# A hybrid attention block on Trainium2: in the dilated stage, TensorE's transposes move ahead of its score products

## Chip, cores, metric

The kernel runs on one core of one Trainium2 chip. The metric is the device time of one execution in microseconds, as the median of several runs; lower is better.

## What is computed

One layer over 2048 positions of width 1024. A combined input projection feeds two mixers of eight heads each (head size 64) and a gate; their outputs are gated, projected and normalised. The change is in mixer A, the dilated attention. It runs three configurations on each head, (window, dilation) = (128, 1), (512, 4), (2048, 16):

```python
def fold(a):                       # position t = m*dil + r
    a = a.reshape(b, tc, dil, h, dh).transpose(0, 2, 1, 3, 4)
    ...
    return a.reshape(b, dil, nb, BLK, h, dh)
...
s = jnp.einsum('brnqhd,brnkhd->brnhqk', qf, kf) / math.sqrt(dh) + bias
s = jnp.where(valid[:, None], s, -jnp.inf)     # band of 128 keys, causal
m = jnp.max(s, axis=-1, keepdims=True)
p = jnp.exp(s - m)
den = jnp.sum(p, axis=-1)
o = jnp.einsum('brnhqk,brnkhd->brnqhd', p, vf) / den
...
w = softmax over the three configurations of (m + log den)
y = sum of w * o
```

Each tile of 128 queries sees its own block of 128 keys and, unless it is the first of its residue, the block before it.

## The kernel before

The program is four phases one after the other, with a barrier between them: `front_phase` (first norm and most of the input projection), `stick_phase` (mixer B and the rest of the projection), `dilated_phase` (mixer A) and `output_phase`. Each engine has its own instruction list in a phase, written out by hand, and the lists meet only through semaphores.

In `dilated_phase` a head has 48 tiles, 16 for each configuration. `make_bunches` puts them into 20 bunches: the 4 bunches of dilation 16 (four tiles of one key block each), then 8 of dilation 4, then 8 of dilation 1 (two tiles each, with one or two key blocks). A bunch is at most 512 columns of scores. Two heads make a turn of 40 steps (`STEPS`); there are four turns (`PAIRS`), so 160 steps. The first turn is written out, the others are a loop on the engines, and `run_turns` goes through the steps for TensorE, ScalarE and VectorE alike. Below, S(b), T(b), V(b) and so on mean the work for bunch b.

At step s each engine works on several bunches at once (`behind` gives the bunch that lies a lag behind, across turns too):

- **TensorE** (`one_step`, lines 1335 to 1343): the scores S(s) (`scores`, lines 1294 and 1295; two products for each tile, with the queries as weights, read with the dilation as stride), the transposes T(s-2) (`transpose_weights`, line 1303; three or four), the value products V(s-4) (`values`, lines 1320 and 1321; two for each key block). At step 13 of each turn but the first, `transpose_pair` (line 1331) turns the merged output of the turn before.
- **VectorE**: `minima` (line 1418) reads the scores, adds the bias and takes the row minimum of the negated scores; `add_halves` (line 1436) for bunch s-5; `low_part` (line 1428) makes PT_lo(s-2); at step 13 four times `apply_gate` (line 1475), which waits for an earlier store of y.
- **ScalarE**: `copy_low` (line 1375) for bunch s-5; `high_part` (line 1367) makes PT_hi(s-2) from the transposes; `weights` (line 1358) makes the exponentials of bunch s, each followed by a read of its row sum.
- **SyncE** stores and reloads the rows of the dilated configurations, loads the next head and stores y; **GpSimd** merges the three configurations.

The waits that matter here: S(s) waits until `minima` has read bunch s-2 (`min_done`; the scores have two PSUM banks). T(b) waits for the exponentials of bunch b (`exp_done`) and for `low_part` of bunch b-2 (`lo_done`; two banks again). V(b) waits for `low_part` of b. The exponentials of b wait for `minima` of b.

Of the kernel before, what the change touches and what calls it, by code (L numbers as in the profile page):

```python
# [37 lines left out]
def at(it, per_turn, n):  # L38

    return it * per_turn + n  # L40


def behind(it, before, s, steps, lag):


    if s >= lag:
        return (it, s - lag) if s - lag < steps else None
    return None if before is None else (before, s - lag + steps)
# [1044 lines left out]
def dilated_phase(nc, qk_hi_d, qk_lo_d, gate_d, va_d, toe_d, ident, y_d):  # L1093
# [42 lines left out]
    STEPS = TURN_HEADS * NB  # L1136
    OBANKS = 3 * NTILE // 4

    def bank_of(c, idx):

        return ORDER.index(c) * (NTILE // 4) + idx // 4


    LAG_T, LAG_H, LAG_L, LAG_V, LAG_O = 2, 2, 2, 4, 5
# [8 lines left out]
    with ExitStack() as stack:  # L1153
# [43 lines left out]
        def run_turns(eng, one_step):  # L1197

            for s in range(STEPS):
                one_step(0, None, s)  # L1200
            with eng.Fori(1, PAIRS) as it:
                for s in range(STEPS):
                    one_step(it, it - 1, s)
            for s in range(STEPS, STEPS + max(LAG_O, LAST_WEIGH + 2)):
                one_step(PAIRS - 1, None, s)
# [69 lines left out]
        @block.tensor  # L1275
        def _(pe):
            pe.sem_inc(pt_done, SCORE_SLOTS)
            pe.sem_inc(pv_done, PART_SLOTS)
            pe.sem_inc(y_done, NCH)
            pe.wait_ge(q_zeros_set, 2)  # L1280

            def scores(it, b):
                par, bunch = b // NB, BUNCHES[b % NB][0]
                if b % NB == 0:
                    pe.wait_ge(qk_loaded[par], at(it, 16 * HeadTiles.QK_LOADS, 16 * HeadTiles.QK_LOADS))
                pe.wait_ge(min_done, at(it, STEPS, b + 1))
                for c, idx, r, n, nk, col in bunch:
                    d = DILATIONS[c]
                    q0 = r + d * P * n
                    k0 = r + d * P * (n - nk + 1)  # L1290
                    q = slice(q0, q0 + d * (P - 1) + 1, d)
                    k = slice(k0, k0 + d * (nk * P - 1) + 1, d)
                    out = s_ps[b % 2][:, col:col + nk * P]
                    pe.matmul(out, q_hi2[par][:, q], k_both[par][:, k], start=True, stop=False)  # L1294
                    last = pe.matmul(out, q_lo0[par][:, q], k_both[par][:, k], start=False, stop=True)  # L1295
                last.then_inc(s_done, 1)

            def transpose_weights(it, b):
                width = BUNCHES[b % NB][1]
                pe.wait_ge(exp_done, SCORE_SLOTS + at(it, STEPS, b + 1))  # L1300
                pe.wait_ge(lo_done, at(it, STEPS, b + 1))
                for col in range(0, width, P):
                    last = pe.transpose(t_ps[b % 2][:, col:col + P], prob[b % SCORE_SLOTS][:, col:col + P], ident[:])
                last.then_inc(pt_done, 1)

            def values(it, b):
                par, bunch = b // NB, BUNCHES[b % NB][0]
                pe.wait_ge(lo_done, 2 + at(it, STEPS, b + 1))
                for c, idx, r, n, nk, col in bunch:
                    bank = par * OBANKS + bank_of(c, idx)  # L1310
                    if idx == 0:
                        pe.wait_ge(v_loaded[c][par], at(it, 16 * V_LOADS[c], 16 * V_LOADS[c]))
                    if idx % 4 == 0:

                        pe.wait_ge(rows_done, at(it, 2 * OBANKS, bank + 1))
                    out = o_ps[bank % 2][:, (idx % 4) * P:(idx % 4 + 1) * P]
                    for kb in range(nk):
                        w = slice(col + kb * P, col + (kb + 1) * P)
                        vk = v[c][par][:, idx - nk + 1 + kb, :]
                        pe.matmul(out, PT_hi[b % PART_SLOTS][:, w], vk, start=(kb == 0), stop=False)  # L1320
                        last = pe.matmul(out, PT_lo[b % PART_SLOTS][:, w], vk, start=False, stop=(kb == nk - 1))  # L1321
                last.then_inc(pv_done, 1)

            def transpose_pair(pair, last_pair=False):
                pe.wait_ge(merged, 1 + at(pair, 2, 1 if last_pair else 2))
                for ch in range(NCH):
                    if last_pair:
                        pe.wait_ge(last_merged, ch + 1)
                    pe.wait_ge(gated, at(pair, NCH, ch + 1))
                    for j in range(4):  # L1330
                        last = pe.transpose(y_ps[ch % 2][:, j * P:(j + 1) * P],
                                            y_pos[:, ch * 4 + j, :], ident[:])
                    last.then_inc(y_done, 1)

            def one_step(it, before, s):
                if s < STEPS:
                    scores(it, s)
                if then := behind(it, before, s, STEPS, LAG_T):
                    transpose_weights(*then)
                if then := behind(it, before, s, STEPS, LAG_V):  # L1340
                    values(*then)
                if s == PAIR_AT and before is not None:
                    transpose_pair(before)

            run_turns(pe, one_step)
            transpose_pair(PAIRS - 1, last_pair=True)

# [490 lines left out]
```

## Time and profile before

| what | value |
|---|---|
| median of 3 runs | 1833.44 us (1826.37 to 1836.2) |
| the profiled execution, its own time | 1834.93 us |
| its span, first to last instruction | 1833.1 us |
| TensorE busy | 1706.5 us, 93% |
| VectorE busy | 1173.7 us, 64% |
| ScalarE busy | 806.1 us, 44% |
| dilated stage, first to last product of the 160 steps | 1227.34 to some 1619 us of the span |
| mean granted TensorE clock | 0.967 of full |

Times in the trace are microseconds from the start of the span. "Busy" for TensorE is the time in which any matmul is under way; matmuls overlap, so what a matmul costs in a dense stretch is the distance from its start to the next start, and not its duration. PE is TensorE, PEld its weight loads, DVE VectorE, ACT ScalarE, POOL GpSimd, SPq the queue that SyncE issues DMAs on. The span leaves out 1.8 us of the execution's own time.

### The profile page before, as it was taken

What the parts mean: (1) busy time and instruction counts of PE and PEld (TensorE: products, weight loads), DVE (VectorE), ACT (ScalarE), POOL (GpSimd) and SP (SyncE); (2) the same over time, 40 slices, a digit from 0 to 9 for tenths busy, and PEclk for the clock granted to TensorE, in tenths of its full rate; (3) what the DMA queues carried; (4) which work ended last, traced back from release to release, by engine and by line L of the source; (5) the groups of instructions that cost most, each with busy time, mean ns of one, the idle gap of its engine ahead of it and who ended that gap; (6) DMA issues with size and microseconds to landing.
All of it is one profiled execution on the core that took longest, in us unless ns stands there. A gap on an engine that the chain in (4) does not pass through costs nothing. (4 is left out here: it accounts for less than half of the span.)

```text
span 1833.1 us, 27600 instructions
## 1 busy us (share of the span) xinstructions
PE 1706.5 (93%) x9138; PEld 1457.2 (79%) x9138; DVE 1173.7 (64%) x2323; ACT 806.1 (44%) x1993; POOL 194.7 (11%) x172
## 2 busy tenths in 40 slices
PE   5799999999979999999999999959989899959998
PEld 4577888888868888888787888849989899947886
DVE  5531123333238888888888888837667676765996
ACT  3341112222225555555555555538768686742000
POOL 2102100000000000000000000010222222200231
PEclk9899999999989999999999999979989999979999
DMA  4316954666367539465654454259888888446541
GB/s 161 138 66 222 333 193 166 208 200 209 131 188 221 179 124 289 141 179 177 228 178 150 144 157 153 89 140 204 191 213 180 198 183 195 106 135 216 187 151 59
DMA packets 235236, 320.01 MB, mean 175 GB/s; under 512 B 66781, under 2 KB 160408, under 8 KB 231516
## 3 DMA queue, kind: packets, MB, share of 16 engines
q1 hardware_dynamic: 230620, 308.90, 56.5%
q0 software_dynamic: 2400, 9.48, 1.6%
q8 instruction: 63, 1.03, 0.2%
q14 instruction: 73, 0.60, 0.1%
q10 hardware_dynamic: 2080, 0.01, 0.1%
HBM read 208.38 MB, written 109.94 MB: 174 GB/s over the span
## 5 line engine op out<-in xcount | busy, mean ns | idle before, releaser
L1003 ACT ACTIVATE WT_hi<-wt_ps 128x512 fp32r<-128x512 f32 (+1 forms) x320 | 170.9, 534 | 316.3 <-PE wt_ps L935 316.3
L1049 DVE TENSOR_TENSOR_SCAN W<-w,W,zeros 128x512 f32<-128x512 f32 x192 | 248.2, 1293 | 59.3 <-ACT w L995 58.5
L376 PE MATMUL proj<-h_hi,w_hi 128*128 128x512 f32 x640 | 260.2, 407 | 19.2 <-DVE h_lo L552 16.5
L376 PE MATMUL proj<-h_hi,w_lo 128*128 128x512 f32 x640 | 253.2, 396 | 0.0
L376 PE MATMUL proj<-h_lo,w_hi 128*128 128x512 f32 x640 | 252.9, 395 | 0.0
L1358 ACT ACTIVATE prob<-neg_s,rows 128x256 f32<-128x256 f32 (+1 forms) x384 | 173.5, 454 | 51.8 <-DVE rows L1418 47.9
L1057 DVE TENSOR_TENSOR WT_lo<-wt_ps,WT_hi 128x512 fp32r<-128x512 f32 (+1 forms) x320 | 187.4, 586 | 2.2 <-ACT WT_hi L1003 2.2
L1294 PE MATMUL s_ps<-k_both,q_hi 128*128 128x256 f32 (+1 forms) x384 | 151.9, 402 | 38.1 <-DMA q_lo<-qk_lo_d 20.1
L1418 DVE CUSTOM_DVE_ANT_0 neg_s<-s_ps,bias 128x256 f32<-128x256 f32 (+1 forms) x384 | 122.6, 363 | 99.5 <-PE s_ps L1295 89.3
L935 PE MATMUL wt_ps<-ident,W 128*128 128x128 f32 x1088 | 173.5, 275 | 7.0 <-DVE WT_lo L1057 6.2
L995 ACT ACTIVATE w<-z_ps 128x512 f32<-128x512 f32 (+2 forms) x320 | 169.3, 529 | 19.4 <-PE z_ps L925 19.4
L935 PEld LDWEIGHTS wt_ps<-ident,W 128*128 128x128 f32 x1088 | 131.7, 140 | 43.6 <-DVE WT_lo L1057 15.7
L971 PE MATMUL proj_a<-h_hi,wa_hi 128*128 128x512 f32 x384 | 152.3, 397 | 9.5 <-DMA wa_lo<-wa_d 9.5
L376 PEld LDWEIGHTS proj<-h_hi,w_hi 128*128 128x128 f32 x640 | 122.4, 191 | 46.5 <-DVE h_lo L552 18.2
L971 PE MATMUL proj_a<-h_lo,wa_hi 128*128 128x512 f32 x384 | 152.8, 398 | 0.0
L1320 PE MATMUL oa_ps<-va,PT_hi 128*128 128x128 f32 x600 | 151.7, 289 | 0.7 <-DVE rows L1436 0.7
L971 PE MATMUL proj_a<-h_hi,wa_lo 128*128 128x512 f32 x384 | 151.8, 395 | 0.0
L1321 PE MATMUL oa_ps<-va,PT_lo 128*128 128x128 f32 x600 | 146.3, 280 | 0.0
L1049 DVE TENSOR_TENSOR_SCAN W<-w,ones_above 128x128 f32<-128x128 f32 (+3 forms) x128 | 114.5, 895 | 47.2 <-ACT w L995 46.0
L376 PEld LDWEIGHTS proj<-h_hi,w_lo 128*128 128x128 f32 x640 | 122.4, 191 | 27.0
L954 PE MATMUL o_ps<-WT_hi,dv 128*128 128x512 f32 (+1 forms) x320 | 142.2, 444 | 0.0
L376 PEld LDWEIGHTS proj<-h_lo,w_hi 128*128 128x128 f32 x640 | 122.7, 192 | 23.3
(134 smaller groups left out, 3355.4 us busy)
## 6 DMA issues: line engine op xcount, KB each, us to landing
wa_hi<-wa_d SPq DMA_DIRECT2D x48, 512.0 KB, 3.9
wa_lo<-wa_d SPq DMA_DIRECT2D x48, 512.0 KB, 5.0
va<-va_d SPq DMA_DIRECT2D x32, 512.0 KB, 11.4
wa_d<-x_sb SPq DMA_DIRECT2D x24, 512.0 KB, 3.8
w_raw<-in_w_tiles SPq DMA_DIRECT2D x18, 512.0 KB, 5.1
moved<-move_d SPq DMA_DIRECT2D x16, 528.0 KB, 4.2
x_sb<-in_x SPq DMA_DIRECT2D x16, 512.0 KB, 5.9
qk_hi_d<-st SPq DMA_DIRECT2D x32, 256.0 KB, 2.8
```

The source lines that it names most:

```text
L376: last = pe.matmul(acc[n % ACC_SLOTS][:], w[w_slot(t)][:, k, :], h[ch][:, k, :], start=(k, a) == (0, 0), stop=(k, a) == (KD - 1, 2))
L935: last = pe.transpose(t_ps[n % T_SLOTS][:, i * P:(i + 1) * P], W[(QB * u + i) % W_SLOTS][:, j * P:(j + 1) * P], ident[:])
L954: pe.matmul(o[:, cols], dv[h % 2][:, c * QB + j, :], WT_hi[n % PART_SLOTS][:, cols], start=False, stop=False)
L971: last = pe.matmul(acc[a % 2][:], wt[a % 2][:, k, :], ht[ch % 2][:, k, :], start=rest == 0, stop=rest == KD * 3 - 1)
L995: act.activation(w[n % W_IN][:, 0:width], z_ps[n % Z_SLOTS][:, 0:width], ACT.Sigmoid, scale=-SCALE).then_inc(w_done, 1)
L1003: act.activation(WT_hi[n % PART_SLOTS][:, cols], t_ps[n % T_SLOTS][:, cols], ACT.Copy) \
L1049: dve.tensor_tensor_scan(W[n % W_SLOTS][:, 0:width][:, ::-1], w[n % W_IN][:, 0:width][:, ::-1], above[:, ::-1], first, ALU.mult, ALU.max). ...
L1057: dve.tensor_tensor(WT_lo[n % PART_SLOTS][:, cols], t_ps[n % T_SLOTS][:, cols], WT_hi[n % PART_SLOTS][:, cols].bitcast(F32), ALU.subtract) ...
L1294: pe.matmul(out, q_hi2[par][:, q], k_both[par][:, k], start=True, stop=False)
L1320: pe.matmul(out, PT_hi[b % PART_SLOTS][:, w], vk, start=(kb == 0), stop=False)
L1321: last = pe.matmul(out, PT_lo[b % PART_SLOTS][:, w], vk, start=False, stop=(kb == nk - 1))
L1358: last = act.activation(prob[b % SCORE_SLOTS][:, col:col + nk * P], neg_s[b % SCORE_SLOTS][:, col:col + nk * P], ACT.Exp, scale=-1.0, bias ...
```

## The change

In TensorE's step, the call of `transpose_weights` is put ahead of the call of `scores`. Nothing else differs; the other engines' lists are the same.

```diff
             def one_step(it, before, s):
+                if then := behind(it, before, s, STEPS, LAG_T):
+                    transpose_weights(*then)
                 if s < STEPS:
                     scores(it, s)
-                if then := behind(it, before, s, STEPS, LAG_T):
-                    transpose_weights(*then)
                 if then := behind(it, before, s, STEPS, LAG_V):
                     values(*then)
```

The first place where TensorE's list differs is step 2 of the stage. In the piece of the difference below, the rows without a sign are the end of S(1) and the start of S(2); `s_ps` are the banks of the scores, `pt_ps` those of the transposes, `prob` the exponentials.

```order
 L1294 MATMUL s_ps1<-k_both0,q_hi20 128x128
 L1295 MATMUL s_ps1<-k_both0,q_lo00 128x128
+L1303 MATMUL pt_ps0<-ident,prob0 128x128 [waits pt_lo_done,exp_done]
+L1303 MATMUL pt_ps0<-ident,prob0 128x128 x3
 L1294 MATMUL s_ps0<-k_both0,q_hi20 128x128 [waits min_done]
 L1295 MATMUL s_ps0<-k_both0,q_lo00 128x128
```

T(0), with its wait for the exponentials, now stands between S(1) and S(2); before, it stood behind S(2).

The second place is step 16 of a turn in the loop, on TensorE, in dilation 1, three steps behind `transpose_pair`. The first row is the end of V(11) (`oa_ps` are the banks of the value products), and before the change the list reads:

```order
L1321 MATMUL oa_ps1<-va1_0,PT_lo3 128x128
L1294 MATMUL s_ps0<-k_both0,q_hi20 128x256 [waits min_done]
L1295 MATMUL s_ps0<-k_both0,q_lo00 128x256
L1294 MATMUL s_ps0<-k_both0,q_hi20 128x256
L1295 MATMUL s_ps0<-k_both0,q_lo00 128x256
L1300 REGISTER_ALU
L1303 MATMUL pt_ps0<-ident,prob2 128x128 [waits pt_lo_done,exp_done]
L1303 MATMUL pt_ps0<-ident,prob2 128x128 x3
L1315 REGISTER_ALU [waits va0_loaded0,pt_lo_done]
L1320 MATMUL oa_ps0<-va0_0,PT_hi0 128x128 [waits rows_done]
```

With the change:

```order
L1321 MATMUL oa_ps1<-va1_0,PT_lo3 128x128
L1300 REGISTER_ALU
L1303 MATMUL pt_ps0<-ident,prob2 128x128 [waits pt_lo_done,exp_done]
L1303 MATMUL pt_ps0<-ident,prob2 128x128 x3
L1294 MATMUL s_ps0<-k_both0,q_hi20 128x256 [waits min_done]
L1295 MATMUL s_ps0<-k_both0,q_lo00 128x256
L1294 MATMUL s_ps0<-k_both0,q_hi20 128x256
L1295 MATMUL s_ps0<-k_both0,q_lo00 128x256
L1315 REGISTER_ALU [waits va0_loaded0,pt_lo_done]
L1320 MATMUL oa_ps0<-va0_0,PT_hi0 128x128 [waits rows_done]
```

T(14) and its wait now stand ahead of S(16), and S(16) stands between T(14) and V(12).

## Rows read from the trace of the kernel before

**Rows 1.** Busy time by stretch: us, PE, PEld, DVE, ACT, POOL, clock, DMA share, GB/s
```profile
1402.38:1415.93 13.55, 13.55 (x123) 13.55 (x122) 12.14 (x45) 13.28 (x45) 0.00 (x0) 1.00 1.05 255
1371.92:1415.93 44.01, 44.01 (x324) 43.74 (x323) 33.16 (x141) 36.73 (x130) 10.44 (x5) 1.00 0.85 186
1361.87:1368.31 6.44, 6.44 (x30) 6.24 (x31) 5.16 (x18) 5.46 (x19) 0.00 (x0) 0.52 0.89 267
1227.34:1636.60 409.26, 375.76 (x2632) 369.20 (x2632) 284.40 (x1156) 293.34 (x1032) 73.09 (x35) 0.93 0.79 177
```

**Rows 2.** Waits of 1227 to 1640: us in total, times, longest
```profile
ACT PT_hi L1367 <- PE pt_ps L1303: 45.1, 69, 2.3
DVE ya_out L1475 <- DMA y_d<-ya_out: 23.6, 3, 8.5
...
PE s_ps L1294 <- DVE rows L1418: 18.0, 3, 6.7
```

**Rows 3.** Timeline of PE, one step of dilation 1: start, duration, what
```profile
1412.32 0.33 PE L1294 MATMUL s_ps<-k_both,q_hi 128*128 128x256 f32 x1
...
1412.84 0.60 PE L1303 MATMUL pt_ps<-ident,prob 128*128 128x128 f32 x4
1413.20 0.31 PE L1320 MATMUL oa_ps<-va,PT_hi 128*128 128x128 f32 x1
...
1414.12 0.33 PE L1294 MATMUL s_ps<-k_both,q_hi 128*128 128x256 f32 x1
```

**Rows 4.** Timeline of the weight loads in the same step
```profile
1412.61 0.19 PEld L1295 LDWEIGHTS s_ps<-k_both,q_lo 128*128 128x128 f32 x1
1412.74 0.46 PEld L1303 LDWEIGHTS pt_ps<-ident,prob 128*128 128x128 f32 x4
1413.17 0.19 PEld L1320 LDWEIGHTS oa_ps<-va,PT_hi 128*128 128x128 f32 x1
```

**Rows 5.** Timelines of ACT and PE: last read of a bunch, and a step's start
```profile
1385.69 0.19 ACT L1358 ACTIVATION_READ_ACCUMULATOR prob<-neg_s,rows 128x1 f32 x1
...
1386.52 0.55 PE L1294 MATMUL s_ps<-k_both,q_hi 128*128 128x256 f32 x1
...
1406.48 0.19 ACT L1358 ACTIVATION_READ_ACCUMULATOR prob<-neg_s,rows 128x1 f32 x1
...
1407.12 0.33 PE L1294 MATMUL s_ps<-k_both,q_hi 128*128 128x256 f32 x1
```

**Rows 6.** Timelines of PE and ACT, start of the stage
```profile
1227.34 0.46 PE L1294 MATMUL s_ps<-k_both,q_hi 128*128 128x128 f32 x1 [20.11 <-DMA q_lo<-qk_lo_d]
...
1231.92 0.19 ACT L1358 ACTIVATION_READ_ACCUMULATOR prob<-neg_s,rows 128x1 f32 x1
...
1232.59 1.06 PE L1303 MATMUL pt_ps<-ident,prob 128*128 128x128 f32 x4
1233.31 0.46 PE L1294 MATMUL s_ps<-k_both,q_hi 128*128 128x128 f32 x1
...
1235.79 0.46 PE L1294 MATMUL s_ps<-k_both,q_hi 128*128 128x128 f32 x1
...
1236.87 1.03 PE L1303 MATMUL pt_ps<-ident,prob 128*128 128x128 f32 x4
1237.56 0.45 PE L1320 MATMUL oa_ps<-va,PT_hi 128*128 128x128 f32 x1
...
1238.88 0.55 PE L1294 MATMUL s_ps<-k_both,q_hi 128*128 128x256 f32 x1
```

**Rows 7.** Timelines of PE, its loads and ACT behind the second turn's stop
```profile
1361.87 0.58 PE L1294 MATMUL s_ps<-k_both,q_hi 128*128 128x256 f32 x1 [6.65 <-DVE rows L1418]
...
1362.75 0.19 ACT L1358 ACTIVATION_READ_ACCUMULATOR prob<-neg_s,rows 128x1 f32 x1
...
1362.99 0.71 PEld L1303 LDWEIGHTS pt_ps<-ident,prob 128*128 128x128 f32 x4 [0.20 <-ACT prob L1358]
...
1365.08 0.52 PE L1294 MATMUL s_ps<-k_both,q_hi 128*128 128x256 f32 x1
```

## Prediction

> **What bounds the kernel now.** I read the busy times by stretch first, since the change lies in one stage. The reader is to see that the dilated stage is some 409 us of the span with TensorE busy for 375.76 us of it, and that within one whole head, 1371.92 to 1415.93, TensorE is busy for all of 44.01 us at full clock, with ScalarE at 36.73 us and VectorE at 33.16 us [rows 1]. Eight heads of 44.01 us are 352 us: most of the stage is a stream of TensorE work without a hole. The tightest stretch for the others is dilation 1 (1402.38 to 1415.93), where ScalarE is busy for 13.28 of 13.55 us.
>
> Second, the waits of the stage: TensorE has only three long ones for VectorE, 18.0 us in all, and VectorE waits just as often for a store of y, 23.6 us in all [rows 2]. These are the stops of `apply_gate` at step 13 of turns two to four; a DMA ends them. ScalarE waits 69 times for transposes, 45.1 us, but while TensorE has no hole that costs nothing.
>
> Third, the timeline of TensorE in a step of dilation 1: S starts at 1412.32, T at 1412.84, V at 1413.20, the next S at 1414.12 [rows 3]. So S costs 0.52 us, T 0.36, V 0.92, the step 1.80.
>
> **The change, part by part.** Per step, the same matmuls are issued, four transposes ahead of the scores instead of behind them. No DMA and no instruction of another engine moves. There are four costs to weigh.
>
> *The seams between the groups.* Before, the order in a ring is S, T, V; now T, S, V. The weight loads show what a seam costs: last load of S at 1412.61, first of T at 1412.74 (0.13 us), the four loads of T and the seam to V 0.43 us (0.11 each) [rows 4]. The step's 16 loads take 1.80 us, 0.11 each, so a seam is worth 0.02 us at most. Whether S to V, V to T and T to S are dearer or cheaper than the old seams no row shows; 0.02 us in 160 steps bounds it at 3.2 us either way. I take 0.
>
> *The new wait in the dense steps.* T(s-2) now begins its step, so the exponentials of s-2 must be done by the step's start. In the trace of before I compared, for each of the 20 steps of the head at 1371.92, the end of the last row-sum read of bunch b with the start of step b+2. The smallest distance is 0.45 us (twice, and 0.46 once), in dilation 1: the read at 1406.48 ends at 1406.67, and the step starts at 1407.12. At the seam from dilation 16 to 4 it is 0.64 us (1385.88 against 1386.52), elsewhere mostly 0.7 to 1.3 [rows 5]. With the change S itself ends later within its step by the length of T, 0.36 us, and where ScalarE is not the one that is behind, the exponentials come later by as much. That leaves 0.45 - 0.36 = 0.09 us, of which the signal takes 0.05 (behind a stop, the exponentials end at 1362.75 + 0.19 = 1362.94 and T starts at 1362.99 [rows 7]). So the wait is met, but only just. I take 0.6 us in all: 0.07 us for each head, for the one or two steps that may miss by a few hundredths. Below, it cannot be less than 0. Above, ScalarE bounds it: in dilation 1 it has 13.28 us of work in 13.55 us, so each bunch in which it falls behind makes TensorE wait, by what the rival below prices. `lo_done`, the other wait of T, is a step older and not near.
>
> *The start of the stage.* Before, T(0) stood behind S(2), and TensorE had three bunches of scores to hide the first exponentials. From S(0) at 1227.34 to the end of the exponentials of bunch 0 (1231.92 + 0.19 = 1232.11) it takes 4.77 us [rows 6]. S of a bunch costs 5.25 / 3 = 1.75 us here, T 0.72 (1232.59 to 1233.31), S(4) 1.08, T(2) 0.69, V(0) 1.32. With the change: S(0) and S(1) end at 1230.84, T(0) waits until 1232.16 (1.3 us of idle TensorE), S(2) starts at 1232.88, T(1) at 1234.63, S(3) at 1235.35 and ends at 1237.10. The exponentials of bunch 2 end 4.77 us behind the start of S(2), at 1237.65, so T(2) starts at 1237.70, after 0.6 us more of waiting. Then S(4) at 1238.39, V(0) at 1239.47, step 5 at 1240.79. Before, step 5 began at 1238.88: **+1.9 us**. If the clock rises at the same time as before, V(0) is quicker and it is 1.5.
>
> *The restart behind each stop.* When the gate is through, VectorE first makes the minima of bunch 14. Before, S(16) started on them at 1361.87, while ScalarE made the exponentials; T(14) followed at 1362.99 and had waited for ScalarE for 0.20 us; step 17 came at 1365.08 [rows 7]. With the change TensorE can do nothing until those exponentials are done: T(14) starts at the same 1362.99, and S(16), which took 1.1 us at 0.52 of the clock [rows 1, 7], comes behind it. All that follows moves by 1.0 us. The end of the stop itself is set by the DMA and does not move against the work before it. Three stops: **+3.0 us**. Bounds: 0, if a shorter stop gave it back, and 1.1 each.
>
> The last turn's end I cost at nothing: T(159) has the exponentials of the last bunch to wait for either way, and behind it VectorE waits for a DMA. Without that cover it would be the length of T, 0.36 us.
>
> Sum: 0 + 0.6 + 1.9 + 3.0 = **5.5 us**. The profiled execution took 1834.93 us, which makes 1840.4. It lay 1.5 us above the median of 1833.44, so for a median I predict **1839.0 us**, 0.3% more. A measurement of this kernel can tell about 0.5%, or 9.2 us, from no change, so this counts as the same.
>
> A rule speaks against this change. The order puts short idle moments in front of groups of matmuls, and in the rows the clock is 1.00 through a dense head and 0.52 behind a stop of 6.65 us. The Trainium skill (TensorE: Matmul & The Clock Gate, "A second HAM failure mode: psum-queue depth-cycling") says that an engine that idles briefly between groups of matmuls can swing between the two clock levels. By that rule the sum would be that of the last rival below; by the rows it stays as it is, since the idle moments I find in dense steps are under 0.1 us.
>
> **The rivals.**
>
> *Slower: ScalarE sets the pace of dilation 1.* The ring is now exponentials, T, S, minima, exponentials, all within two steps, and the margin of 0.09 us is made of differences of rows. If it is missed steadily, from some 0.1 us on, TensorE waits in each of the 8 steps of dilation 1 in 8 heads. At 0.1 to 0.25 us for each of 64 steps that is 6.4 to 16 us, and with the sum 1846 to 1855 us. For it: ScalarE's 13.28 of 13.55 us. Against: the margins are of the trace itself, ScalarE's work per step is the same, and its transposes come earlier, which lets it run ahead.
>
> *Nothing at all.* The stops are ended by a DMA whose loads were issued some eight steps earlier. If these do not follow TensorE's delays but the memory, the start's and restart's losses are swallowed by the next stop. Then only the last restart and the steps behind it count, 1.0 us: 1834.5. Against: the loads are issued when a head's rows are done, so they follow TensorE.
>
> *Faster: the new seams are cheaper.* If the strided weight loads of S hid better behind transposes than behind value products, each step could give something back. To be faster by over 0.5% it would take (9.2 + 5.5) / 160 = 0.09 us a step, more than four times the seam seen. With the bound of 3.2 us the result is 1833.44 + 5.5 - 3.2 = 1835.7, still the same.
>
> *The clock falls.* At 0.52 of the clock, a step of dilation 1 took 3.21 us (1361.87 to 1365.08) against 1.80. If the gaps brought the clock down in 64 steps, that would be 1.41 x 64 = 90 us: 1929 us.
>
> **How the numbers follow.** Forecast 0.57, ScalarE's pace 0.22, nothing at all 0.14, cheaper seams 0.05, clock 0.02. The likeliest gives 1839.0. Of the forecast's chance some 0.04 lies beyond 9.2 us, so slower by over 0.5% is 0.22 + 0.02 + 0.04 = 0.28; faster by over 0.5% I put at 0.05, seams and the scatter of medians together; the rest, 0.67, is within. The range runs from 1831, the 1834.5 of no effect less the 3 us by which the three runs scatter, to 1853, most of the first rival; it leaves out the top of that, the clock and the far seams, under 0.2.
>
> **What the new profile should show.** In a dense head, steps of 1.80 us in dilation 1 as before, and TensorE busy without a hole; waits of transposes for `prob` many but in sum under 1 us there. At the start two waits, 1.3 and 0.6 us, and step 5 some 13.5 us behind S(0) instead of 11.5. Behind each stop, T first and S 0.7 us later, and step 17 1.0 us later after the minima of bunch 14. ScalarE's wait for transposes should fall well below 45.1 us, and part of it turn up as waits for the minima. The prediction is wrong if transposes wait for `prob` in most steps of dilation 1, if the clock in a dense head is below 1.00, or if a dense head is not 44.0 us long.

## The result, and the profile after

| | before | after |
|---|---|---|
| median, same chip | 1833.12 us (14 runs, 1826.37 to 1837.73) | 1839.72 us (14 runs, 1834.05 to 1842.7) |
| the profiled execution | 1834.93 us | 1839.46 us |
| its span | 1833.1 us | 1837.7 us |
| mean granted clock of the span | 0.967 | 0.963 |

The ratio is 1.0039, with a 95% interval of [1.0027, 1.0051]: a small loss, clear of no change, and smaller than the 0.5% below which the forecast counts two kernels as the same. A second series of the same kernel gave 1.004 [1.0026, 1.0053]. The forecast of 1839.0 us and "the same" held. Its sum did not hold in all its terms: the start was too small, one place was missing altogether, and time that the forecast took as lost was in part given back. The profile of before lay 1.8 us above its median and that of after 0.3 us below, so the two profiles are only 4.5 us apart.

First the busy times by stretch of the changed kernel, the same columns as [rows 1]: the eight steps of dilation 1, the whole head around them, the stage.

```profile
1402.79:1416.35 13.56, 13.56 (x123) 13.46 (x122) 12.09 (x45) 12.84 (x44) 0.08 (x1) 1.00 1.10 273
1372.49:1416.35 43.86, 43.86 (x324) 43.55 (x323) 32.85 (x141) 35.45 (x130) 10.45 (x5) 1.00 0.88 190
1227.38:1641.00 413.62, 376.78 (x2632) 370.52 (x2632) 280.88 (x1156) 285.90 (x1032) 73.22 (x36) 0.91 0.77 175
```

The dense head takes 43.86 us against 44.01 before, TensorE has no hole in it and the clock is 1.00. TensorE's busy time in the stage grew by 1.0 us and the clock went from 0.93 to 0.91. The loss is not in the stream of dense steps.

Second, the waits of the stretch 1220 to 1645 (us in total, times, longest), against [rows 2].

```profile
DVE neg_s L1418 <- PE s_ps L1295: 109.2, 109, 20.9
ACT prob L1358 <- DVE rows L1418: 108.1, 99, 16.2
PE pt_ps L1303 <- ACT prob L1358: 22.0, 7, 8.0
DVE ya_out L1475 <- DMA y_d<-ya_out: 21.9, 3, 8.6
...
DVE neg_s L1418 <- issue: 7.2, 3, 3.0
...
ACT PT_hi L1367 <- PE pt_ps L1303: 5.2, 5, 1.5
```

ScalarE's waits for transposes fell from 45.1 us to 5.2; it now idles 99 times for the minima instead (108.1 us). TensorE waits for the exponentials seven times, and these seven are all of it: two at the start of the stage, three behind the stops, two at the starts of turns three and four. Those last two are not in the forecast.

Third, the place where the exponentials come nearest to the transposes that need them: the last row-sum read of bunch 11 on ScalarE, then the last value product and T(11) on TensorE. Behind it stands a step of dilation 1 on TensorE, to set beside [rows 3].

```profile
1404.07 0.18 ACT L1358 ACTIVATION_READ_ACCUMULATOR prob<-neg_s,rows 128x1 f32 x1
```

```profile
1404.12 0.27 PE L1321 MATMUL oa_ps<-va,PT_lo 128*128 128x128 f32 x1
1404.31 0.66 PE L1303 MATMUL pt_ps<-ident,prob 128*128 128x128 f32 x4
...
1412.79 0.62 PE L1303 MATMUL pt_ps<-ident,prob 128*128 128x128 f32 x4
1413.17 0.36 PE L1294 MATMUL s_ps<-k_both,q_hi 128*128 128x256 f32 x1
...
1413.72 0.22 PE L1320 MATMUL oa_ps<-va,PT_hi 128*128 128x128 f32 x1
...
1414.57 0.62 PE L1303 MATMUL pt_ps<-ident,prob 128*128 128x128 f32 x4
```

T costs 0.38, S 0.55, V 0.85, the step 1.78 us (before 1.80). The exponentials of bunch 11 end at 1404.25 and T(11) starts 0.05 us later, which is the time of the signal [rows 7]. From the value product before it to T(11) it is 0.19 us, where the transposes of most steps start 0.11 us behind the product before them. So T(11) does wait, by 0.08 us, and T(13) by 0.07 us (1407.63, again 0.05 us behind its exponentials); the other 18 steps of this head don't. No idle time shows, because the product before still runs. The next smallest distance is 0.10 us.

Fourth, all places where TensorE waits for the exponentials and what VectorE did before three of them. The number in brackets is the idle time before the row and what ended it; "issue" is idle time in which the engine waited for nothing that the profile shows. First TensorE.

```profile
1232.20 1.12 PE L1303 MATMUL pt_ps<-ident,prob 128*128 128x128 f32 x4 [1.12 <-ACT prob L1358]
1237.81 1.12 PE L1303 MATMUL pt_ps<-ident,prob 128*128 128x128 f32 x4 [0.40 <-ACT prob L1358]
...
1363.18 1.12 PE L1303 MATMUL pt_ps<-ident,prob 128*128 128x128 f32 x4 [7.95 <-ACT prob L1358]
1363.95 0.56 PE L1294 MATMUL s_ps<-k_both,q_hi 128*128 128x256 f32 x1
...
1366.12 1.07 PE L1303 MATMUL pt_ps<-ident,prob 128*128 128x128 f32 x4
...
1422.76 0.66 PE L1303 MATMUL pt_ps<-ident,prob 128*128 128x128 f32 x4 [0.17 <-ACT prob L1358]
1463.89 1.12 PE L1303 MATMUL pt_ps<-ident,prob 128*128 128x128 f32 x4 [7.51 <-ACT prob L1358]
1522.95 0.66 PE L1303 MATMUL pt_ps<-ident,prob 128*128 128x128 f32 x4 [0.45 <-ACT prob L1358]
1566.00 0.87 PE L1303 MATMUL pt_ps<-ident,prob 128*128 128x128 f32 x4 [4.41 <-ACT prob L1358]
```

And VectorE, the gate of the first stop, the first minima of turns three and four, the gate of the last stop.

```profile
1359.92 1.39 DVE L1475 TENSOR_TENSOR ya_out<-y_ps,gate_a 128x512 f32<-128x512 f32 x2 [8.62 <-DMA y_d<-ya_out]
1420.01 0.29 DVE L1418 CUSTOM_DVE_ANT_0 neg_s<-s_ps,bias 128x128 f32<-128x128 f32 x1 [2.73 <-issue]
1520.20 0.29 DVE L1418 CUSTOM_DVE_ANT_0 neg_s<-s_ps,bias 128x128 f32<-128x128 f32 x1 [3.02 <-issue]
1562.76 1.38 DVE L1475 TENSOR_TENSOR ya_out<-y_ps,gate_a 128x512 f32<-128x512 f32 x2 [5.09 <-DMA y_d<-ya_out]
```

The waits at the start and the restart look as forecast (1.12 and 0.40 us; T first, S 0.77 us behind it). The row at 1522.95 is small, but what follows it is not. The busy times by stretch from there on (PEclk is the third number from the end) show it.

```profile
1515.80:1522.95 7.15, 6.70 (x46) 6.55 (x45) 4.09 (x23) 4.29 (x18) 0.00 (x0) 1.00 0.85 147
1522.95:1530.84 7.89, 7.89 (x41) 7.89 (x41) 3.84 (x20) 5.16 (x22) 0.00 (x0) 0.65 0.45 77
1530.84:1537.64 6.80, 6.80 (x33) 6.80 (x34) 3.67 (x18) 4.43 (x18) 0.00 (x0) 0.50 0.34 81
1537.64:1543.50 5.86, 5.86 (x32) 5.85 (x33) 3.53 (x17) 3.25 (x12) 3.92 (x3) 0.59 1.03 224
```

Behind a wait of 0.45 us TensorE is busy without a hole, yet at 0.65, 0.50 and 0.59 of the clock, that is partly and then wholly at the lower of its two levels, until 1543.5. The Trainium skill (TensorE: Matmul & The Clock Gate, "A second HAM failure mode: psum-queue depth-cycling") says that short idle moments between groups of matmuls, when they come often, can swing the clock. Here the trace agrees that a short one can be followed by a fall, and here one was enough; for the 64 steps of dilation 1 at which the forecast had held it as a rival, the trace does not bear it out.

**Where the 4.5 us of the two profiles went.** I took the start of S(s) in both traces, less the start of S(0) of that trace, and read off how far after is behind before. From mark to mark (S stands behind T in its step, so the first mark holds 0.36 us that are no loss):

| stretch | how far after falls behind, us |
|---|---|
| start of the stage to step 20 | +3.75 |
| second head of the first turn, up to the first stop | -3.44 |
| first stop and the six steps around it | +0.60 |
| start of turn three up to its stop | +0.29 |
| second stop | +0.44 |
| start of turn four up to its stop | +5.58 |
| third stop | -2.27 |
| dense stretches between (three) | -0.38 |
| sum | +4.57 |

### The profile page after: what moved, and what is told of

It is laid out like the page before. It is cut to its first block and busy times, and to the rows that moved or that the text cites. A ratio compares the mean times of both kernels' runs of the same rounds, so it can differ in the third digit from the quotient of the medians.

```text
span 1837.7 us, 27600 instructions
## 1 busy us (share of the span) xinstructions
PE 1708.4 (93%) x9138; PEld 1459.1 (79%) x9138; DVE 1170.0 (64%) x2323; ACT 798.4 (43%) x1993; POOL 194.9 (11%) x172
## 5 line engine op out<-in xcount | busy, mean ns | idle before, releaser
L1358 ACT ACTIVATE prob<-neg_s,rows 128x256 f32<-128x256 f32 (+1 forms) x384 | 173.5, 453 | 109.0 <-DVE rows L1418 108.1
L1294 PE MATMUL s_ps<-k_both,q_hi 128*128 128x256 f32 (+1 forms) x384 | 156.0, 413 | 20.1 <-DMA q_lo<-qk_lo_d 20.1
L1320 PE MATMUL oa_ps<-va,PT_hi 128*128 128x128 f32 x600 | 143.1, 274 | 0.0
```

The lines of the kernel that those rows point to most:

```text
L1358: last = act.activation(prob[b % SCORE_SLOTS][:, col:col + nk * P], neg_s[b % SCORE_SLOTS][:, col:col + nk * P], ACT.Exp, scale=-1.0, bias ...
```

## The experiments

All kernels compute everything. What is changed is the place of T in some steps, or how the loop is written. Ratios are against the kernel before, timed on the same chip, with the 95% interval.

**One place put back.** The first three kernels are the changed kernel with the old order in a few steps. Only the condition differs: `before is None` is the first turn.

```diff
-                if then := behind(it, before, s, STEPS, LAG_T):
+                scores_first = before is None and s < 5            # start
+                scores_first = before is not None and s == 16      # restart
+                scores_first = before is not None and s < 5        # turn
+                then = behind(it, before, s, STEPS, LAG_T)
+                if then and not scores_first:
                     transpose_weights(*then)
                 if s < STEPS:
                     scores(it, s)
+                if then and scores_first:
+                    transpose_weights(*then)
```

Old order at the start of the stage alone:

> The changed kernel with the old order (scores, then transposes) put back in steps 0 to 4 of the first turn alone. Theory (the lost cover at the start, the restarts and the turn starts each cost something, and a clock that falls or rises late multiplies it): the first transposes come 5.25 us behind S(0) again, step 5 is 11.5 us behind S(0) and not 13.9, and the clock is at full by about 11 us behind S(0) and not 17. But the first turn of the kernel before then ran into a wait of VectorE for the reloaded rows at the second head (1285 to 1297 of its span), and the changed kernel did not; so the stop should come back and most of the 3.4 us be lost again there: the third head then starts within 1 us of where the changed kernel has it, ratio 1.002 to 1.004. Rival (the start's loss goes straight to the end): 3.4 us less than the changed kernel, ratio about 1.002.

Old order in step 16, behind the stops:

> The changed kernel with the old order put back in step 16 of the turns in the loop alone, the step behind each stop. Theory: behind each stop S(16) starts as soon as the minima of bunch 14 are there, T(14) waits 0.2 us or less behind it, and step 17 begins 3.2 us behind S(16) as before, so 1.0 us is won at each of three stops: ratio about 1.002 against 1.004 for the changed kernel. The other losses stay: two waits at the start, and at the start of turns 3 and 4 a wait of the transposes for the exponentials of 0.1 to 0.5 us. Rival (the clock, and not the order behind the stop, is what counts): no difference from the changed kernel in time, since the work behind the stop is done at the same half clock.

Old order in steps 0 to 4 of turns two to four:

> The changed kernel with the old order put back in steps 0 to 4 of the turns in the loop alone, where VectorE stands idle for some 3 us before the first minima of a turn. Theory: TensorE no longer waits for the exponentials at the start of turns 3 and 4 (0.17 and 0.45 us in the changed kernel), the clock stays at full through the first head of the fourth turn (it was at half for some 16 us), and the time falls by about the 5.6 us that the first eight steps of that turn had lost, as far as the DMA stop behind them does not give it back: ratio 1.000 to 1.002, mean clock 0.965 or more in most runs. Rival (the clock fell by chance there, and does so in any kernel): the waits go but the clock still falls in some first head, and the ratio stays at 1.004.

Measured: start 1.0023 [1.0013, 1.0033], restart 1.0012 [0.9999, 1.0026], turn 1.0007 [0.9998, 1.0016]. Each took something of the 1.0039 away, and by the middle values, whose intervals overlap, the place that was not in the forecast took the most. With the old order at the turns' starts no wait and no fall of the clock was left there, and the clock of the span was 0.970. In the second kernel the wait at the start of turn three was 0.45 us this time, and there the clock fell; that of turn four was 0.16 us, and it did not. For the first kernel I had also expected that, with the start's loss gone, VectorE's wait for reloaded rows at the second head would return. It did not (the value products waited 0.08 us there), and the clock rose 15.4 us behind S(0) and not 11: these were misses. The ratio fits the rival's 1.002 as well as the theory's.

**All three put back.** `scores_first = s < 5 or (before is not None and s == 16)`: what remains of the change is the new order in the other steps.

> The changed kernel with the old order put back in the three places together: steps 0 to 4 of every turn, and step 16 of the turns in the loop. The new order stays in the other steps, which are dense. Theory: each of the three costs is gone and what is left is the cheaper seam, 0.15 us a head (43.86 us against 44.01): no wait of the transposes for the exponentials over 0.1 us, a stage 1 to 2.5 us shorter than in the kernel before, ratio 0.998 to 1.000, at least 3 us less than each of the kernels with one place put back. Rival (the dense steps of the new order cost something too, because their margin is under 0.1 us): ratio 1.001 or more, and waits of the transposes in dilation 1.

Measured: 1.0002 [0.999, 1.0014]. Within the interval the whole cost lies in these few steps, and no cost of the new order in the dense ones can be seen. The expectation that it would take at least 3 us less than each of the one-place kernels held against the first of them only.

**One place alone.** The converse: the kernel before, with the new order only in steps 0 to 4 of turns two to four, only in step 16, or only in steps 0 to 4 of the first turn (the condition above, negated).

> The kernel before, with the new order in steps 0 to 4 of the turns in the loop alone, where VectorE stands idle for some 3 us before the first minima. Theory: the transposes of step 2 wait for the exponentials by 0.1 to 0.5 us at the start of turns 3 and 4, and where that is some 0.4 us or more the clock falls to half for the next ten or more us, at 2 to 6 us each; so a ratio of 1.001 to 1.004, with a wider scatter than the kernel before. Rival (the clock falls by chance): the waits cost their 0.5 us and the ratio is 1.000.

> The kernel before, with the new order in step 16 of the turns in the loop alone. Theory: S(16) comes 0.7 us behind T(14) instead of on the minima, step 17 is 1.0 us later after the end of each stop, less what a clock that rises at the same moment gives back (0.4 us of it as the changed kernel's profile has it): 1.8 to 3.0 us in all, ratio 1.001 to 1.0016. Rival (a DMA ends the next stop too, so that it swallows the loss): under 1 us, ratio 1.000.

> The kernel before, with the new order in steps 0 to 4 of the first turn alone. If the start costs what the marks of the changed kernel say (3.0 to 3.9 us by step 9) and nothing gives it back: a ratio of 1.0017 to 1.0021, and the clock rising some 6 us later than before. Rival (the start's loss is swallowed at the second head, where VectorE waits for reloaded rows): below 1.0008, with a shorter wait of VectorE there than in the kernel before.

Measured: turn 1.0022 [1.0005, 1.0039], restart 1.0017 [1.0007, 1.0027], start 1.0023 [1.0011, 1.0036]. The timelines of VectorE and TensorE in the first of them, at the start of turn four and its stop:

```profile
1522.84 0.29 DVE L1422 CUSTOM_DVE_ANT_0 neg_s<-s_ps,bias 128x128 f32<-128x128 f32 x1 [3.93 <-issue]
1525.59 0.66 PE L1303 MATMUL pt_ps<-ident,prob 128*128 128x128 f32 x4 [1.10 <-ACT prob L1362]
...
1565.09 1.29 DVE L1479 TENSOR_TENSOR ya_out<-y_ps,gate_a 128x512 f32<-128x512 f32 x2 [2.64 <-DMA y_d<-ya_out]
1567.12 0.39 PE L1294 MATMUL s_ps<-k_both,q_hi 128*128 128x256 f32 x1 [0.74 <-DVE rows L1422]
```

VectorE idles 3.93 us, T waits 1.10, and the clock is 0.50 from 1531 to 1549. By step 14 this turn was 8 us later than at its start; then the stop, whose end the DMA sets, was 0.74 us for TensorE and not 5.48 as in the kernel before. The clock stayed at 1.00 behind it, where the kernel before ran at the lower level, and by step 19 of the turn 6.9 us were given back. In turn three of the same execution VectorE idled 2.80 us, T did not wait, the clock stayed.

The second kernel shows the restart by itself. From the gate's first row to the next step is 6.18 us at turns two and three (1365.00 to 1371.18 and 1465.87 to 1472.05), against 5.33 before (1359.75 to 1365.08 [rows 7]): 0.85 us at each of the two (0.85 at turn four as well).

In the third, the clock of the first stretches (1227 to 1232, then 6 us each) decides:

```profile
1238.00:1244.00 6.00, 6.00 (x28) 6.00 (x29) 3.83 (x19) 4.22 (x16) 0.00 (x0) 0.50 1.10 216
1244.00:1250.00 6.00, 6.00 (x30) 6.00 (x29) 2.59 (x11) 3.26 (x12) 0.00 (x0) 0.50 1.01 218
1250.00:1256.00 6.00, 6.00 (x30) 6.00 (x29) 3.01 (x13) 3.32 (x11) 0.00 (x0) 0.50 1.01 306
1256.00:1262.00 6.00, 6.00 (x42) 5.94 (x41) 3.88 (x16) 4.18 (x13) 0.00 (x0) 0.94 1.16 239
```

Before, the stretch from 1238 to 1244 had 0.97. Here the clock rose only at about 1256.7 (0.94 in the last stretch: 0.06 / 0.50 of 6 us at the lower level), 18 us later, though TensorE had no hole from 1238 on. At step 20 the kernel was 6.87 us behind. Against the profile of before, which had a wait and a fall of the clock of its own at the second head, it kept 3.65 us of it to the first stop and 1.40 to the end of the stage. Against the profile of before's written-out form (below), which had no such fall, it kept 6.07 and 4.52. The ratio says 4.2 us. So a part is swallowed later, but the rival, which wanted a ratio below 1.0008, is refuted.

**The same kernel again.**

> The changed kernel once more, for a second profile and as a control beside the others. Theory: waits of the transposes for the exponentials of 1.1 and 0.4 us at the start, of 3 to 8 us at the three stops, and of 0.1 to 0.5 us at the start of turns 3 and 4; in which of these turns the clock falls to half goes with the size of that wait (0.45 us: it falls; 0.17 us: it does not). Ratio 1.003 to 1.005. Rival (clock by chance): the clock falls where there was no wait, or stays with a wait of 0.4 us or more.

Measured: 1.004 [1.0026, 1.0053]. The fall of the clock moved: in turn three VectorE idled 3.02 us, T waited 0.45 and the clock fell to 0.50; in turn four 2.65, T came 0.10 us late, and the clock did not fall. So the place is fixed and its size varies from execution to execution.

**The loop written out.** What is VectorE idle for? At the start of turns three and four it and ScalarE take the jump back of the loop; the other candidate was the four DMAs that SyncE issues there. This kernel writes the three turns out on VectorE and ScalarE, and leaves the order of the change.

```diff
-        def run_turns(eng, one_step):
+        def run_turns(eng, one_step, unroll=False):
...
-            with eng.Fori(1, PAIRS) as it:
-                for s in range(STEPS):
-                    one_step(it, it - 1, s)
+            if unroll:
+                for it in range(1, PAIRS):
+                    for s in range(STEPS):
+                        one_step(it, it - 1, s)
...
-            run_turns(act, one_step)
+            run_turns(act, one_step, unroll=True)
...
-            run_turns(dve, one_step)
+            run_turns(dve, one_step, unroll=True)
```

> The changed kernel with the loop over turns 2 to 4 written out on VectorE and ScalarE (their lists have no jump back); TensorE keeps its loop and the new order. Theory (VectorE's idle of 2.7 to 3.9 us ahead of the first minima of turns 3 and 4, for which the trace names no releaser, is the jump back to the loop's start): the idle is gone or under 1 us, no wait of the transposes for the exponentials at a turn's start, clock 1.00 through the first heads of turns 3 and 4, and 3 to 5 us less than the changed kernel: ratio about 1.001. The waits at the start and behind the stops stay. Rival (the idle comes from the four DMAs that SyncE issues at that moment, line 1248): it stays at some 3 us, and so does the ratio of 1.004.

```profile
1521.84 0.29 DVE L1423 CUSTOM_DVE_ANT_0 neg_s<-s_ps,bias 128x128 f32<-128x128 f32 x1 [1.69 <-issue]
```

Measured: 1.0012 [1.0, 1.0023]. VectorE's idle time at the start of turns three and four is 1.69 us, as at other heads' starts in this kernel, no transposes wait at a turn's start, and the clock stays. The expectation of under 1 us was a miss. The four DMAs of SyncE were still issued, at 1520.52, 1.3 us ahead of the minima. So the idle time beyond 1.69 us goes with the jump and not with the DMAs. In the control below the same minima wait 1.54 us, and the trace names the scores as what ended it, so the rest is likely a wait for the scores. Its control is the same edit on the kernel before:

> The kernel before with the same loop written out on VectorE and ScalarE, as the control of the run beside it. Theory: there the idle was hidden behind the scores of the next bunch, so taking it away changes nothing: ratio 0.999 to 1.001. Rival (fetching a longer list costs the engines or the DMA queues something): ratio above 1.001.

Measured: 1.0006 [0.9992, 1.002] at a median of 1831.51 us against 1832.62. No difference can be told, and in the trace of before no TensorE work waits at a turn's start: S covered the jump, so that its length did not matter.

**T last.** If being ahead of S is what exposes T, the far end of the step should be the safest place: S, V, T.

> Scores, values, then transposes: the same ring as in the changed kernel (each seam is the same), but the transposes come at the end of their step, so that their cover is longer than in the kernel before. Theory: a dense head takes 43.86 us as in the changed kernel and not 44.01 (the new seams are cheaper by 0.15 us a head), no wait of the transposes for the exponentials at the start, at turn starts or behind a stop, and so 1 to 3 us less than the kernel before: ratio 0.998 to 1.000. Rival (ScalarE or VectorE now gets its work too late: the high part starts a value group later): VectorE and ScalarE have less time up to the value products, and the ratio is over 1.002.

```profile
1336.13 0.33 PE L1320 MATMUL oa_ps<-va,PT_hi 128*128 128x128 f32 x1 [0.53 <-DVE rows L1436]
```

Measured: 1.0041 [1.0027, 1.0054], a clear miss. The value products now wait for `add_halves`, 0.53 us at one step of each of six heads, since the softmax weights of the configurations delay VectorE there. At the second head of the first turn they waited twice, 0.52 and 0.46 us, and the clock fell. At the start of turn four VectorE idled 4.59 us, the scores waited 0.86 us, and the clock fell. Each of the new orders exposes a wait at every head or turn that the old one covers.

**Only the dense steps, loop written out.** The best that the pieces point to: `e4_all`'s condition with the written-out loop.

> The changed kernel with the old order in steps 0 to 4 of every turn and in step 16 of the loop's turns, and the loop of VectorE and ScalarE written out: what is left of the change is the new order in the dense steps, whose heads were 43.86 us instead of 44.01 in the changed kernel. My theory (the change costs only at the start, the stops and the turns' starts, and gains 0.15 us a head elsewhere): 0 to 3 us faster than before, a ratio of 0.9985 to 1.0, and no wait of transposes at a turn's start. Rival (the dense steps cost something too, which the other terms have hidden): 1.0005 or more. A gain of over 3 us would need a cause I have not seen.

Measured: 0.9991 [0.9979, 1.0004], 1831.69 us against 1831.99, no wait of transposes at a turn's start. That fits "0 to 3 us faster" and does not exclude no gain. No version here clearly beats the kernel before.

## Why the prediction held, point by point

**The seams, 0 within 3.2 us.** Right. T, S, V cost 0.38, 0.55 and 0.85 where they had cost 0.36, 0.52 and 0.92 [rows 3], and a dense head is 0.15 us shorter although it holds 0.15 us of new waits. So the seams give 0.3 us a head, an estimate of 2.4 us over eight heads. With 0.015 us a step the rival of the cheaper seams had the direction, at a sixth of the 0.09 us that it needed.

**The wait in dense steps, 0.6 us.** Right in its mechanism and near in its size. Forecast were a margin of 0.09 us, 0.05 of it for the signal, and one or two steps of a head that miss by a few hundredths. The trace has T(11) and T(13) late by 0.08 and 0.07 us in a full head, and the exponentials 0.10 us ahead at the next nearest steps. Over the eight heads that is some 1 us. The rival that ScalarE sets the pace falls: only two steps of twenty are missed, and for the reason given against it. With T first in a step its copies come early, and it waits for the minima (99 times) instead of running behind. (Its 1846 is 1845.3 by its own terms, 1838.9 + 6.4.)

**The start, 1.9 us: mis-sized, by the clock.** The two waits came as forecast. T(0) and T(2) start 4.82 and 10.43 us behind S(0), where 4.82 and 10.36 were forecast; their idle times read 1.12 and 0.40 us and not 1.3 and 0.6 because the product before still runs in part of them. Step 5 began 13.87 us behind S(0), where 13.45 was forecast and 11.54 had been before. The step that failed is the price of what follows: the forecast used the rows of before and considered only "if the clock rises at the same time as before". It rose later. By the mean clock of each stretch, the rise lies 10.7 to 11.2 us behind S(0) in the four profiles with the old start and the old dense steps (before, its written-out form, turn only, restart only), 15.2 to 15.8 us in three with the old start and the new dense steps, and with the new start 15.5 to 15.6 us (three profiles), 18.1 (after), 28.4 and 29.1. The new start costs up to step 20, by the marks, 2.8 us at 15.5, 3.75 at 18.1 and 6.6 to 6.9 at 28.4 to 29.1. The three with the old start and the new dense steps are already 1.6 to 1.8 us behind at step 20, so a part of this goes with the order of the dense steps and not with the two waits. What decides among these times the runs don't show.

**The restart, 1.0 us each: right.** 0.85 us in the kernel with that place alone; in after 0.87, 0.85 and 0.70 at the three stops (1359.92 to 1366.12 is 6.20 us against 5.33). That is 2.4 us where 3.0 were forecast.

**"All that follows moves": only in part.** The rival "nothing at all" had a chance of 0.14, and its mechanism is real. A stop's end follows a DMA. When turn four was 7 us late, the gate came 4.4 us later (1562.76 against 1558.39), VectorE waited 5.09 us where it had waited 7.38, and 2.3 us were back. The second head of the first turn is the other such place: in the profile of before, value products waited 0.71 us at 1287.55 because VectorE had waited for reloaded rows, and the clock was 0.54 from 1290 to 1297; after came later and had none of it. How much of the 3.44 us this gives back differs from execution to execution. Of the four profiles with the old order in the whole first turn, three wait there (0.71, 0.93 and 1.80 us) and the clock falls; the written-out form of before waits 0.32 us, the clock stays, and it takes 24.46 us for the nine steps where before took 26.78. None of the six profiles with the new start waits there. So a late start does ease this place, by an amount that these few profiles don't settle.

**The turns' starts: not in the sum.** This is the step that was missing. The forecast searched the margins of one dense head for the nearest exponentials and took them for all heads. At the head that begins turn three or four, VectorE's idle time is longer by the loop's jump, and S ahead of T had hidden it: the trace of before shows 2.84 and 3.70 us of it and no wait behind. With T first the cover is gone. The waits are 0 to 1.1 us; where they reached 0.45 us the clock fell, and 3.3 to 8 us were lost up to the stop (marks of turn three or four).

| turn's start (order of that place new) | VectorE idle, us | T waits, us | clock |
|---|---|---|---|
| after, turns 3 and 4 | 2.73, 3.02 | 0.17, 0.45 | stays, falls |
| the same again | 3.02, 2.65 | 0.45, 0.10 | falls, stays |
| old order at the stage's start | 2.75, 2.72 | 0.19, 0.16 | stays, stays |
| old order behind the stops | 3.00, 2.72 | 0.45, 0.16 | falls, stays |
| turns' starts alone | 2.80, 3.93 | 0, 1.10 | stays, falls |
| loop written out | 1.69, 1.69 | 0, 0 | stays, stays |

In the five other profiles that have the loop and the old order at this place (before, `e3_turn`, `e4_all`, `e7_restart_only`, `e12_start_only`) VectorE idled 2.7 to 3.7 us at all ten starts, no transposes waited, and the clock stayed at all ten. So the fall goes with TensorE's wait and not with VectorE's idle time.

**The clock rival.** Put at 0.02 for 64 steps and 90 us, it was refused as such, rightly: the clock is 1.00 in the dense heads. But the sentence that the idle moments are under 0.1 us was true of dense steps only, and the rule worked at another place at the price of a few microseconds.

So the total came out right (5.5 us forecast; 6.6 by the medians, of which the start 1.0016 to 1.0023, step 16 1.0017 to 1.0027 and the turns' starts 1.0022 to 1.0032, each measured both alone and by taking it away) through a missing loss and a larger start on one side, and what the stops and the second head gave back on the other. That these came out within about a microsecond is luck; the forecast had bounded neither. That the single effects sum to more than the whole, 0.0062 or 0.0075 against 0.0039, agrees with the giving back, though it doesn't show it: the intervals of some 0.0010 to 0.0017 each leave room.

## What to carry to other kernels

When a group of instructions is moved ahead of another, ask at every irregular place (the first steps, a restart, the jump of a loop, the step with an extra piece) what the other group had been covering there; the margin of the steady steps says nothing about them. Price a short wait of TensorE by the clock of the stretch behind it and not by its own length alone. And where a later stop is ended by a transfer, expect part of any earlier loss back, and compare medians rather than two profiles when the effect is a few microseconds.

## What the runs showed of the hardware

- **Short waits and the clock.** In front of work of dilation 16 at a turn's start, waits of 0.45 us (three times), 0.86 and 1.10 us were each followed by a fall to the lower clock, and waits of 0.10 to 0.19 us (five) were not. In the steps of dilation 4, waits of 0.71, 0.93 and 1.80 us were followed by a fall, and so was a pair of 0.52 and 0.46 us (T last); one of 0.32 us, a pair of 0.53 and 0.35 us (`e4_all`) and six single ones of 0.53 us (T last; the clock was 1.00 from 1336.13 to 1348) were not. In dilation 1, behind the last stop of `e5_turn_only`, waits of 0.74 and 0.39 us were not. The length of a wait alone does not decide.
- **What the lower clock costs** depends on the work. The score products of dilation 16 start 0.22 us apart at 0.50 (1227 to 1231 of before) and at 1.00 (1372 to 1374), while the value products start 0.22 us apart at 0.50 (1290.08 of T last) and 0.11 at 1.00 (1287.05).
- **The rise.** With the same kernel the clock rose 15.6 or 18.1 us behind the stage's first product, and 28.4 and 29.1 us in two others with the same start, though TensorE had no idle time behind the second of the two waits, 10.4 us behind that product.
- **A jump back of a loop.** VectorE was idle for 2.65 to 4.59 us ahead of its first instruction behind the jump, where the written-out code had 1.28 to 1.54 us (old order there) or 1.69 (new). It varies between executions of one kernel (2.73 and 3.02; 3.02 and 2.65).
- **Signals.** The exponentials' end to the transposes' start is 0.05 us on the path, read behind the stop [rows 7] and again at T(11) and T(13) of the changed kernel's dense head.
